# One block of modulation sums moved to VectorE, and attention scores as three reduced-precision products

## The chip, the cores and the metric

The kernel runs on one core of a Trainium2 chip. The metric is the device time of one execution in microseconds. Three executions of the kernel before took 1014.57, 1015.67 and 1015.83 us, median 1015.67.

## The reference

Two transformer blocks over one sequence of 256 rows of 1024 values, in fp32. What matters here lies at the head of the first block:

```
mod_x = silu(c) @ w_mod + b_mod            # 1024 -> 6 * 1024, one row of condition c
mod_c = silu(c_ctx) @ w_mod + b_mod        # the same for the context's condition
sh_m, sc_m, gt_m, sh_f, sc_f, gt_f = split(mod_x, 6)
hx, hc = modulate(rms_norm(x), sh_m, sc_m), modulate(rms_norm(ctx), csh_m, csc_m)
qa, ka, va, qr, kr, vr, gr = split(h @ w_in)          # for hx and for hc
att = softmax(q k^T * 64**-0.5) v                     # 8 heads of 64, 2 key heads, 256 + 256 keys
ret = bidir_retention(qr, kr, vr, decays, states of the context)
x1 = x + gt_m * rms_norm(concat(att, norm(ret) * silu(gr)) @ w_out)
x2 = x1 + gt_f * rms_norm(swiglu(modulate(rms_norm(x1), sh_f, sc_f)))
```

The first two parts of the modulation (sh_m, sc_m) are needed for both conditions before anything can be projected. The last two (sh_f, gt_f, the third group below) are needed only for `c`, and only after attention.

## The kernel before

All large products are made of a high and a low part of fp32: `w = w_hi + w_lo`, `x = x_hi + x_lo`, each part of type fp32r, and `x w` is the sum of hi·hi, hi·lo and lo·hi (function `three`, L1818 to L1820), 128x128 by 512 columns each. The weights come as 148 units of 1 MB (128 x 2048). For a unit v: SyncE loads it into one of three `raw` slots, ScalarE writes `w_hi` (L641), VectorE writes `w_lo = raw - w_hi` (L1156, called by `low_to`), TensorE uses both. A unit of `raw` is loaded again when its `w_lo` is there, and `w_hi` is written again when TensorE has used the unit.

Each engine runs a list written out by hand, and waits on semaphores; the order of the lists is the order of the work. TensorE's list after the first units is: unit W_IN+2 and +3 (values of retention, `vr`, four row tiles), +4 (`kava`: keys and values of attention), +5 and +6 (`qa`), +7 and +8 (`qr`), +9 and +10 (`gr`). Between them stand the visits of the modulation: 24 units of 1 MB of `w_mod`, in three groups of eight. `mod_unit` (L1924) multiplies one by `silu_c` (128 x 32) in plain fp32, in four strips of 512 columns that go to four column strips of the array and to 32 rows each of one PSUM bank; the trace shows each fp32 matmul as two records. Group 0 is done early, groups 1 and 2 in the visits: two units before W_IN+2's context half, then three after each of the next units, at last two; the third group is visited after the units W_IN+3 (three), W_IN+4 (three) and W_IN+5 (two). `mod_row_out` copies a group's bank, `mod_T` (L1933) transposes it, `mod_columns` (L1278) adds the bias. Twelve of these units are loaded into two places of their own (`memV`, `qrn_qan`), four through the `raw` ring.

After unit W_IN+5 TensorE makes the context's states (`states`, L2058 and L2066), which wait for `kr_done` and for four tiles of centred values (`centre_values`, L1336 to L1338, VectorE). At unit W_IN+9 it transposes the attention queries (`queries_T`, L1903), which need VectorE's two ropes over them (six ropes done in all), makes the first tile of the unit, and then the scores of the first two of eight pairs (`scores`, L2093): for each pair two fp32 matmuls, 64 rows by 128, 512 columns, key head 0 in partitions 0 to 63 and key head 1 in 64 to 127, each to its own bank. VectorE takes the maxima (L1420), ScalarE the exponentials (L834), VectorE normalises (L1432), TensorE transposes (L2217) and weights (L2168).

VectorE's list in this stretch: `w_lo` of W_IN+4; `w_lo` of W_IN+5 and W_IN+6; the block keys (L1349) and sixteen steps of decay arguments (L1354, L1358); the four centrings, with `mod_columns(1)` between; squares and norms of `ka`, `w_lo` of W_IN+7, two ropes; the states' copy (L1387); `w_lo` of W_IN+8; sums over `qa` (L1396); `w_lo` of W_IN+9; `mod_columns(2)`; norms and ropes of `qa`; `w_lo` of W_IN+10; ropes of `qr`; the first maxima. `chain` makes an instruction end before the next begins.

Of the kernel before, what the change touches and what calls it, by code (L numbers as in the profile page):

```python
# [37 lines left out]
P = 128  # L38
T = 256
# [42 lines left out]
VISITS = {W_IN + 2: 2, W_IN + 3: 3, W_IN + 4: 3, W_IN + 5: 3, W_IN + 6: 3, W_IN + 7: 2}  # L82
# [12 lines left out]
assert _m == N_MOD  # L95
STREAM += [("w", v) for v in range(W_REG, N_W)]
HEAD_UNITS = W_REG + N_MOD - MOD_K - len(OWN_MODS)
# [98 lines left out]
def plan_banks():  # L196
# [40 lines left out]
    plan.signalled(("modT", 1), 5)  # L237
    plan.streamed(("mod_row", 2), 7)
# [92 lines left out]
def two_blocks_kernel(nc, io):  # L331
# [5 lines left out]
    def sem(name):  # L337
        if name not in named:
            named[name] = sems.enter_context(nc.semaphore(name))
        return named[name]  # L340

    with sems, stack:
# [45 lines left out]
        ARENA = 18440  # L388
        spot = ExitStack()
# [8 lines left out]
        sums_r = spot.enter_context(nc.sbuf_tensor("sums_r", [P, LEVELS + 2, P], F32R))  # L398
        spot.close()
# [14 lines left out]
        qaT, kaT = carve(0, PAIRS, T), carve(1024, 4 * P)  # L414
# [24 lines left out]
        silu_gr = carve(at, TB, 512); tables = carve(at, 4, TB * HD); at += 1024  # L439
        ka_all = carve(at, 4, P); at += 512  # L440
# [57 lines left out]
        own_mods = [memV[:].rearrange("p b d -> p (b d)"), qrn_qan]  # L498
        hi_ready = sem("hi_ready")
# [70 lines left out]
        def _(sp):  # L570
# [9 lines left out]

            sp.dma_start(cols[:], io["cols"]).then_inc(sem("cols_loaded"), 16)
# [20 lines left out]
            for u in range(W_IN + 2, HEAD_UNITS):  # L602
                unit_in(u)
                kind, v = STREAM[u]
                if kind == "w" and v in VISITS:
                    for n, (m, (at, slot)) in enumerate(OWN_MODS.items()):
                        if at == v:
                            sp.wait_ge(mod_used, mods_behind(v)[0])
                            sp.dma_start(own_mods[slot], io["own_mods"][n]).then_inc(sem(f"own_mod_loaded{slot}"), 16)
                if u == RAW_AT[("w", W_IN + 2)]:  # L610
                    sp.dma_start(const1, io["const1"]).then_inc(sem("const1_loaded"), 16)
# [24 lines left out]
        def _(act):  # L636
# [85 lines left out]
            def mod_row_out(g):  # L722

                act.wait_ge(mod_used, MOD_K * (g + 1))
# [94 lines left out]
            act.activation(kaT[:, :], b[:, :], ACT.Copy).then_inc(read_sem(("kaT", 0)), 1)  # L819
# [3 lines left out]
            queries_out("qaT", qaT)  # L823
# [316 lines left out]
        def _(dve):  # L1140
# [204 lines left out]
            ins.then_inc(sem("kr_done"), 1)  # L1345
            low_to(W_IN + 5)
            low_to(W_IN + 7)
# [63 lines left out]
            dve.wait_ge(mod_used, N_MOD)  # L1411
# [3 lines left out]
            low_to(W_IN + 11)  # L1415

# [398 lines left out]
        def _(pe):  # L1815
# [111 lines left out]

            def mod_T(g):
# [159 lines left out]
            def scores(p):  # L2088
                j, tb = p // 2, p % 2
                for kv in range(KV_HEADS):  # L2090
                    half = slice(64 * kv, 64 * kv + 64)
                    b = free(pe, ("scores", p, kv))
                    pe.matmul(b[:, :], qaT[half, j, tb * P:(tb + 1) * P], kaT[half, :],  # L2093
                              start=True, stop=True).then_inc(full_sem(("scores", p, kv)), 1)
# [15 lines left out]
            for part, units, tiles in [("vr", 2, both), ("kava", 1, both), ("qa", 2, both[:2]), ("qr", 2, both[:2]),  # L2110
                                       ("gr", 2, both[:2])]:
                for e in range(units):
# [5 lines left out]
                    if j == 4:  # L2118
                        mod_T(1)
# [430 lines left out]
def lay_out(a):  # L2550
# [30 lines left out]
    for at in (512, 0, 1024, 2560, 3072, 2048, 1536):  # L2581
# [25 lines left out]
        "first_mods": np.stack(mods[:MOD_K]), "own_mods": np.stack([mods[m] for m in OWN_MODS]),  # L2607
        "cols": np.concatenate([small[name] for name in COLS], axis=1),
# [21 lines left out]
```

## Time and profile before

| what | us |
|---|---|
| median of three executions | 1015.67 |
| the profiled execution, its own time | 1015.45 |
| its span, first to last instruction | 1013.7 |
| TensorE busy (5164 matmuls) | 995.3 (98%) |
| VectorE busy (660) | 584.6 (58%) |
| ScalarE busy (603) | 495.8 (49%) |
| the chain that ended last, TensorE's share | 93% |

Busy time of TensorE is modelled: a 512-column fp32r matmul is shown as some 0.39 us long but the next one starts 0.23 us after it. The distance of starts is what a matmul costs in a dense row. The granted clock of TensorE was 0.998 of its full speed over the span.

### The profile page before, as it was taken

How to read it: one execution, taken by the hardware profiler on the slowest of the kernel's cores; microseconds unless marked ns; L12 is line 12 of the kernel's file. 1: busy time of each engine (PE TensorE's matmuls, PEld its weight loads, DVE VectorE, ACT ScalarE, POOL GpSimd, SP SyncE). 2: the span in 40 equal slices, each digit the busy share in tenths (PEclk: the TensorE clock that was granted, in tenths of full speed). 3: DMA queues.
4: the chain of work that ended last, by engine and by line, in shares of the span. 5: the costliest groups of instructions: out<-in, count | busy, mean ns of one | idle time of the engine just before them, and what ended most of it. 6: DMA issues, size and time to landing. Idle time of an engine off the chain costs nothing.

```text
span 1013.7 us, 13246 instructions
## 1 busy us (share of the span) xinstructions
PE 995.3 (98%) x5164; PEld 810.6 (80%) x5164; DVE 584.6 (58%) x660; ACT 495.8 (49%) x603; POOL 0.2 (0%) x4
## 2 busy tenths in 40 slices
PE   7999999999999999999999999999999999999997
PEld 5777776778888888888888887888888878888885
DVE  5374768667555554565555665567774465555543
ACT  6473347656544443554444534663545554444432
POOL 0000000000000000000000000000000000000000
PEclk9999999999999999999999999999999999999999
DMA  9967653133655545475545465534244245555441
GB/s 373 419 272 297 274 218 126 43 121 128 213 203 173 199 169 205 166 259 174 199 166 193 166 222 182 195 125 147 102 166 166 81 147 192 198 177 202 166 166 42
DMA packets 26686, 188.32 MB, mean 186 GB/s; under 512 B 2960, under 2 KB 3216, under 8 KB 4112
## 3 DMA queue, kind: packets, MB, share of 16 engines
q1 hardware_dynamic: 26064, 185.24, 50.2%
q10 hardware_dynamic: 576, 2.43, 0.6%
q8 instruction: 34, 0.56, 0.2%
q14 instruction: 12, 0.10, 0.0%
HBM read 186.61 MB, written 1.05 MB: 185 GB/s over the span
## 4 chain that ended last, share of the span: by engine, by line
PE 93%; DMA 2%; DVE 2%; ACT 1%; issue 1%; SPq 1%; ACTq 0%; DVEq 0%
PE bank L1818 24%; PE bank L1820 24%; PE bank L1819 24%; DMA raw<-in_weights 2%; PE bank L2026 2%; PE bank L1862 2%; PE bank L1846 2%; PE bank L1924 2%; PE bank L1854 2%; PE bank L2292 1%; PE bank L1903 1%; PE bank L2390 1%; PE bank L2217 1%; PE bank L2168 1%; PE bank L2093 1%
## 5 line engine op out<-in xcount | busy, mean ns | idle before, releaser
L1156 DVE TENSOR_TENSOR w_lo<-raw,w_hi 128x2048 fp32r<-128x2048 f32 x148 | 338.6, 2291 | 267.6 <-ACT w_hi L641 267.4
L641 ACT ACTIVATE w_hi<-raw 128x2048 fp32r<-128x2048 f32 x148 | 283.7, 1918 | 268.1 <-PE bank L1820 217.4
L1818 PE MATMUL bank<-w_hi,hT_hi 128*128 128x512 f32 (+1 forms) x760 | 299.8, 394 | 0.0
L1820 PE MATMUL bank<-w_hi,hT_lo 128*128 128x512 f32 (+1 forms) x760 | 294.9, 388 | 0.0
L1819 PE MATMUL bank<-w_lo,hT_hi 128*128 128x512 f32 (+1 forms) x760 | 294.3, 387 | 0.0
L1818 PEld LDWEIGHTS bank<-w_hi,hT_hi 128*128 128x128 f32 x760 | 142.8, 188 | 33.0 <-issue 5.7
L1820 PEld LDWEIGHTS bank<-w_hi,hT_lo 128*128 128x128 f32 x760 | 142.7, 188 | 29.8
L1819 PEld LDWEIGHTS bank<-w_lo,hT_hi 128*128 128x128 f32 x760 | 143.0, 188 | 27.8 <-issue 0.2
L1818 PE MATMUL bank<-w_hi,gT_hi 128*128 128x512 f32 x264 | 103.4, 392 | 0.0
L1820 PE MATMUL bank<-w_hi,gT_lo 128*128 128x512 f32 x264 | 102.8, 389 | 0.0
L1819 PE MATMUL bank<-w_lo,gT_hi 128*128 128x512 f32 x264 | 102.7, 389 | 0.0
L1820 PEld LDWEIGHTS bank<-w_hi,gT_lo 128*128 128x128 f32 x264 | 49.6, 188 | 10.4
L1819 PEld LDWEIGHTS bank<-w_lo,gT_hi 128*128 128x128 f32 x264 | 49.6, 188 | 10.2
L1818 PEld LDWEIGHTS bank<-w_hi,gT_hi 128*128 128x128 f32 x264 | 49.6, 188 | 10.0
L918 ACT ACTIVATE arena<-bank,rstd 128x256 f32<-128x256 f32 x44 | 18.4, 470 | 63.5 <-PE bank L1820 63.5
L1570 DVE SCALAR_TENSOR_TENSOR arena<-bank,rstd,arena 128x256 f32<-128x256 f32 x44 | 19.3, 479 | 30.8 <-ACT arena L918 30.8
L1576 DVE TENSOR_TENSOR gT_lo<-bank,gT_hi 128x512 f32 (+1 forms) x33 | 22.8, 690 | 3.2
L1846 PE MATMUL bank<-w_hi,hT_hi 128*128 128x512 f32 x88 | 22.3, 395 | 2.2 <-issue 0.8
L918 ACT ACTIVATE arena<-bank 128x256 f32<-128x256 f32 x22 | 7.2, 381 | 31.7 <-PE bank L1820 31.7
L1862 PE MATMUL bank<-w_lo,hT_hi 128*128 128x512 f32 x88 | 22.0, 392 | 0.2 <-DVE w_lo L1156 0.2
L1854 PE MATMUL bank<-w_hi,hT_lo 128*128 128x512 f32 x88 | 22.1, 393 | 0.0
L719 ACT ACTIVATE arena<-bank 128x512 f32<-128x512 f32 (+1 forms) x18 | 8.7, 553 | 27.2 <-PE bank L1820 23.8
(310 smaller groups left out, 1008.1 us busy)
## 6 DMA issues: line engine op xcount, KB each, us to landing
raw<-in_weights SPq DMA_DIRECT2D x152, 1024.0 KB, 4.8
arena<-in_first_mods SPq DMA_DIRECT2D x8, 1024.0 KB, 14.9
memV<-in_own_mods SPq DMA_DIRECT2D x6, 1024.0 KB, 4.8
arena<-in_own_mods SPq DMA_DIRECT2D x6, 1024.0 KB, 6.9
arena<-in_const ACTq DMA_DIRECT2D x1, 1088.0 KB, 5.1
memV<-in_mem SPq DMA_DIRECT2D x1, 1024.0 KB, 6.4
x_res<-in_x SPq DMA_DIRECT2D x1, 1024.0 KB, 17.5
arena<-in_ctx SPq DMA_DIRECT2D x1, 1024.0 KB, 15.2
```

Source lines behind the costliest of these rows:

```text
L641: act.activation(w_hi[:, v_slot, :], raw[:, u_slot, :], ACT.Copy).then_inc(hi_ready, 1)
L918: act.activation(gate[:, c % 3, tb, :], bank[(c % 3) * 2 + tb][:, 0:256], ACT.Silu, scale=rstd[:, tb:tb + 1] if f else 1.0)\
L1156: ins = dve.tensor_tensor(w_lo[:, v_slot, n], raw[:, u_slot, n], w_hi[:, v_slot, n].bitcast(F32), ALU.subtract)
L1576: dve.tensor_tensor(gT_lo[:, s, :], bank[6][:, :].rearrange("p (a t) -> p a t", t=T), gT_hi[:, s, :].bitcast(F32), ALU.subtract).then_inc( ...
L1818: pe.matmul(out, hi, rhi, start=start, stop=False)
L1819: pe.matmul(out, hi, rlo, start=False, stop=False)
L1820: return pe.matmul(out, lo, rhi, start=False, stop=stop)
L1846: pe.matmul(out[:, :], hT_hi[:, 2 * q + e, tb * P:(tb + 1) * P], weights(w_hi, q, e), start=(first and q == quarters[0] and e == 0), stop= ...
L1854: pe.matmul(out[:, :], hT_lo[:, 2 * q + e, tb * P:(tb + 1) * P], weights(w_hi, q, e), start=False, stop=False)
L1862: ins = pe.matmul(out[:, :], hT_hi[:, 2 * q + e, tb * P:(tb + 1) * P], weights(w_lo, q, e), start=False, stop=(last and q == quarters[1] a ...
L1924: ins = pe.matmul(b[32 * j:32 * j + 32, :], silu_c[:, k, :], w[:, 512 * j:512 * j + 512], start=(k == 0), stop=(k == MOD_K - 1))
L2026: ins = pe.matmul(out[:, :], (lo if x_low else hi)[:, 4 * half + e, tb * P:(tb + 1) * P], w[:, v % RING, e * 512:(e + 1) * 512], start=(st ...
```

## The change

The third group is no longer multiplied by TensorE unit by unit. Its 8 MB are cut into sixteen pieces of 128 x 1024 (`row_mods`: eight for the first 1024 columns, eight for the second), and VectorE multiplies each by the column `silu_c[:, k, 0:1]` and adds it to a running total (`mod_rows`); only the condition `c` is kept. Then four fp32 matmuls with a stationary of ones sum the totals over the partitions (`mod_sums`). The pieces go to four places of 512 KB (the two halves of `memV` and of `qrn_qan`), of which two hold the totals as well. The visits after W_IN+3, +4 and +5 are gone, `mod_T(1)` stands after W_IN+3 instead of W_IN+4 and has another bank.

The scores are three fp32r products of high and low parts. ScalarE writes the high parts in the copies that it made before, VectorE adds three subtractions for the low parts.

```diff
+ROW_SLOTS = [0, 1, 2, 3, 1, 2, 3, 1, 2, 3, 1, 3, 1, 3, 1, 3]
+ROW_LOADS = {W_IN + 6: 12, W_IN + 7: 4}
-    plan.signalled(("modT", 1), 5)
-    plan.streamed(("mod_row", 2), 7)
+    plan.signalled(("modT", 1), 7)
+    plan.signalled(("mod_row", 2), 7)
...
+        row_mod = [mod_sum[:, e * 1024:(e + 1) * 1024] for mod_sum in own_mods for e in range(2)]
... SyncE, behind the load of unit v
+                if kind == "w" and v in ROW_LOADS:
+                    for _ in range(ROW_LOADS[v]):
+                        step = rows_in[0]
+                        rows_in[0] += 1
+                        if row_before(step) < 0:
+                            sp.wait_ge(mod_used, 2 * MOD_K)
+                        else:
+                            sp.wait_ge(sem("mod_step"), row_before(step) + 1)
+                        sp.dma_start(row_mod[ROW_SLOTS[step]], io["row_mods"][step]).then_inc(...)
... ScalarE
-            act.activation(kaT[:, :], b[:, :], ACT.Copy).then_inc(read_sem(("kaT", 0)), 1)
+            act.activation(kaT_hi[:, :], b[:, :], ACT.Copy).then_inc(sem("kaT_hi"), 1)
-            queries_out("qaT", qaT)
+            for q in range(2):
+                b = filled(act, ("qaT", q))
+                act.activation(qaT_hi[...], b[:, :], ACT.Copy).then_inc(sem("qaT_hi"), 1)
... VectorE
+            def mod_rows(a, b):
+                for step in range(a, b):
+                    slot, part, k = ROW_SLOTS[step], step // MOD_K, step % MOD_K
+                    total = row_mod[2 * part]
+                    dve.wait_ge(sem(f"row_loaded{slot}"), 16 * row_loads(step))
+                    if k == 0:
+                        dve.tensor_scalar(total, row_mod[slot], silu_c[:, k, 0:1], None, ALU.mult).then_inc(sem("mod_step"), 1)
+                    else:
+                        dve.wait_ge(sem("mod_step"), step)
+                        dve.scalar_tensor_tensor(out=total, in0=row_mod[slot], scalar=silu_c[:, k, 0:1], in1=total,
+                                                 op0=ALU.mult, op1=ALU.add).then_inc(sem("mod_step"), 1)
             low_to(W_IN + 5)
-            low_to(W_IN + 7)
... block keys and decay arguments
+            low_to(W_IN + 6)
+            mod_rows(0, 12)
+            low_to(W_IN + 7)
             read_out(dve, ("vr", 3))
             for tile in (2, 3):
                 centre_values(tile)
-            mod_columns(1)
             for tile in (0, 1):
                 centre_values(tile)
+            mod_rows(12, ROW_STEPS)
+            mod_columns(1)
... after the queries' ropes
             low_to(W_IN + 11)
+            dve.tensor_tensor(kaT_lo[:, :], bank_of(("kaT", 0))[:, :], kaT_hi[...], ALU.subtract)...
+            for q in range(2):
+                dve.tensor_tensor(half(qaT_lo), bank_of(("qaT", q))[:, :], half(qaT_hi)..., ALU.subtract)...
... TensorE
+            def mod_sums():
+                pe.wait_ge(sem("mod_step"), ROW_STEPS)
+                b = free(pe, ("mod_row", 2))
+                for j in range(4):
+                    ins = pe.matmul(b[32 * j:32 * j + 32, :], ones[:, 0:32], row_mod[2 * (j // 2)][...512 columns...],
+                                    start=True, stop=True)
+                ins.then_inc(full_sem(("mod_row", 2)), 1)
             def scores(p):
                 j, tb = p // 2, p % 2
-                for kv in range(KV_HEADS):
-                    b = free(pe, ("scores", p, kv))
-                    pe.matmul(b[:, :], qaT[half, j, tb * P:(tb + 1) * P], kaT[half, :], start=True, stop=True)...
+                banks = [free(pe, ("scores", p, kv)) for kv in range(KV_HEADS)]
+                for n, (q_part, k_part) in enumerate([(qaT_hi, kaT_hi), (qaT_hi, kaT_lo), (qaT_lo, kaT_hi)]):
+                    for kv in range(KV_HEADS):
+                        half = slice(64 * kv, 64 * kv + 64)
+                        ins = pe.matmul(banks[kv][:, :], q_part[half, j, tb * P:(tb + 1) * P], k_part[half, :],
+                                        start=(n == 0), stop=(n == 2))
-                    if j == 4:
+                    if j == 3:
                         mod_T(1)
-                    if j < 6:
+                    if j == 2:
                         for m in mods_behind(W_IN + j + 2):
                             mod_unit(m)
+                    if j == 5:
+                        mod_sums()
```

## Rows read from the trace of the kernel before

**Rows 1.** The chain that ended last, in order of time: start us, us, what

```profile
103.06 2.71 PE bank L1924 x24
117.92 2.71 PE bank L1924 x24
126.30 2.06 PE bank L2058 x64
130.32 1.85 PE bank L1924 x16
149.72 1.09 ACT arena L719 x2
150.91 1.06 PE bank L1903 x8
154.72 1.92 PE bank L2093 x8
168.33 1.06 PE bank L2093 x4
186.99 0.65 PE bank L2227 x8
```

**Rows 2.** Timeline of VectorE: start, us, engine, line, operation, tiles [idle before <-releaser]

```profile
83.21 2.28 DVE L1156 TENSOR_TENSOR w_lo<-raw,w_hi 128x2048 fp32r<-128x2048 f32 x1
92.34 2.29 DVE L1156 TENSOR_TENSOR w_lo<-raw,w_hi 128x2048 fp32r<-128x2048 f32 x1 [6.85 <-ACT w_hi L641]
107.00 2.29 DVE L1156 TENSOR_TENSOR w_lo<-raw,w_hi 128x2048 fp32r<-128x2048 f32 x1 [12.36 <-ACT w_hi L641]
115.00 0.68 DVE L1336 TENSOR_REDUCE value_mean<-arena 128x8 f32<-128x512 f32 x1
115.71 0.17 DVE L1337 TENSOR_SCALAR value_mean<-value_mean 128x8 f32<-128x8 f32 x1
121.34 0.69 DVE L1370 TENSOR_TENSOR arena<-arena 128x512 f32<-128x512 f32 x1
149.86 0.69 DVE L1260 TENSOR_TENSOR arena<-arena 128x512 f32<-128x512 f32 x1
152.80 0.68 DVE L1253 TENSOR_TENSOR arena<-arena 128x512 f32<-128x512 f32 x1
167.03 1.29 DVE L1420 TENSOR_REDUCE row_max<-bank 128x1 f32<-128x512 f32 x2 [0.50 <-PE bank L2093]
```

**Rows 3.** Timeline of TensorE: two fp32r matmuls in a dense row

```profile
198.67 0.39 PE L1819 MATMUL bank<-w_lo,hT_hi 128*128 128x512 f32 x1
198.90 0.40 PE L1820 MATMUL bank<-w_hi,hT_lo 128*128 128x512 f32 x1
```

**Rows 4.** Timeline of SyncE's queue: when a load is issued

```profile
92.00 0.33 SPq L609 DMA_DIRECT2D memV<-in_own_mods  x1
```

**Rows 5.** DMA issues from 134 to 150: KB each, us from issue to landing

```profile
raw<-in_weights SPq DMA_DIRECT2D x2, 1024.0 KB, 4.7
```

**Rows 6.** DMA issues of the whole span, as rows 5

```profile
out<-xn SPq DMA_DIRECT2D x1, 512.0 KB, 2.7
fixed<-in_fixed SPq DMA_DIRECT2D x1, 128.0 KB, 2.2
```

**Rows 7.** VectorE's groups by form: xcount | busy us, mean ns | idle before

```profile
L1539 DVE SCALAR_TENSOR_TENSOR x_res<-arena,rstd,x_res 128x512 f32<-128x512 f32 x8 | 5.5, 748 | 0.1
L1186 DVE TENSOR_SCALAR xn<-x_res,rstd 128x1024 f32<-128x1024 f32 x2 | 1.5, 754 | 0.1
```

**Rows 8.** One stretch: its length, then busy us of PE, PEld, DVE, ACT, POOL; clock, DMA

```profile
121.34:150.59 29.25, 28.34 (x222) 22.18 (x220) 20.89 (x43) 12.42 (x17) 0.00 (x0) 1.00 0.65 252
```

**Rows 9.** Timeline of ScalarE, as rows 2

```profile
103.10 2.06 ACT L719 ACTIVATE arena<-bank 128x512 f32<-128x512 f32 x4 [7.87 <-PE bank L1820]
169.57 0.70 ACT L834 ACTIVATE arena<-bank,row_max 128x512 f32<-128x512 f32 x1
```

**Rows 10.** The warm-up's matmuls: ns min/median/max, first and last start

```profile
L1989 PE MATMUL bank<-mod_row x8: 592/1061/1222, 4.7 to 10.4; 128*128 128x512 f32 x8
```

More of the change, by code:

```diff
@@ L81 @@
 OWN_MODS = {}
-VISITS = {W_IN + 2: 2, W_IN + 3: 3, W_IN + 4: 3, W_IN + 5: 3, W_IN + 6: 3, W_IN + 7: 2}
+VISITS = {W_IN + 2: 2, W_IN + 3: 3, W_IN + 4: 3}
+ROW_STEPS = 2 * MOD_K
+ROW_SLOTS = [0, 1, 2, 3, 1, 2, 3, 1, 2, 3, 1, 3, 1, 3, 1, 3]
+ROW_LOADS = {W_IN + 6: 12, W_IN + 7: 4}
 W_REG = W_OUT + 2
@@ L398, in two_blocks_kernel @@
         sums_r = spot.enter_context(nc.sbuf_tensor("sums_r", [P, LEVELS + 2, P], F32R))
+        spot.close()
+        qaT_hi = spot.enter_context(nc.sbuf_tensor("qaT_hi", [P, PAIRS, T], F32R))
+        kaT_hi = spot.enter_context(nc.sbuf_tensor("kaT_hi", [P, 4 * P], F32R))
+        kaT_lo = spot.enter_context(nc.sbuf_tensor("kaT_lo", [P, 4 * P], F32R))
+        spot.enter_context(nc.sbuf_tensor("below_qaT_lo", [P, KA_ALL - 2048], F32))
+        qaT_lo = spot.enter_context(nc.sbuf_tensor("qaT_lo", [P, PAIRS, T], F32R))
         spot.close()
@@ L498, in two_blocks_kernel @@
         own_mods = [memV[:].rearrange("p b d -> p (b d)"), qrn_qan]
+        row_mod = [mod_sum[:, e * 1024:(e + 1) * 1024] for mod_sum in own_mods for e in range(2)]
+        row_before = lambda step: max([n for n in range(step) if ROW_SLOTS[n] == ROW_SLOTS[step]], default=-1)
+        row_loads = lambda step: sum(ROW_SLOTS[n] == ROW_SLOTS[step] for n in range(step + 1))
         hi_ready = sem("hi_ready")
@@ L609, in _ @@
                             sp.dma_start(own_mods[slot], io["own_mods"][n]).then_inc(sem(f"own_mod_loaded{slot}"), 16)
+                if kind == "w" and v in ROW_LOADS:
[6 more added lines that the diff above has]
+                            sp.wait_ge(sem("mod_step"), row_before(step) + 1)
+                        sp.dma_start(row_mod[ROW_SLOTS[step]], io["row_mods"][step]).then_inc(sem(f"row_loaded{ROW_SLOTS[step]}"), 16)
                 if u == RAW_AT[("w", W_IN + 2)]:
@@ L722, in mod_row_out @@
             def mod_row_out(g):
[L724 removed]
+                if g == 2:
+                    filled(act, ("mod_row", 2))
+                else:
+                    act.wait_ge(mod_used, MOD_K * (g + 1))
                 if g:
@@ L1415, in _ @@
             low_to(W_IN + 11)
+            dve.wait_ge(sem("kaT_hi"), 1)
+            dve.tensor_tensor(kaT_lo[:, :], bank_of(("kaT", 0))[:, :], kaT_hi[:, :].bitcast(F32), ALU.subtract).then_inc(read_sem(("kaT", 0)), 1)
+            for q in range(2):
+                dve.wait_ge(sem("qaT_hi"), q + 1)
+                half = lambda v: v[:, 2 * q:2 * q + 2, :].rearrange("p a t -> p (a t)")
+                dve.tensor_tensor(half(qaT_lo), bank_of(("qaT", q))[:, :], half(qaT_hi).bitcast(F32), ALU.subtract)\
+                    .then_inc(read_sem(("qaT", q)), 1)
             def negative_max(p):
@@ L1926, in mod_unit @@
                 ins.then_inc(mod_used, 1)
+            def mod_sums():
+                pe.wait_ge(sem("mod_step"), ROW_STEPS)
+                b = free(pe, ("mod_row", 2))
+                for j in range(4):
+                    ins = pe.matmul(b[32 * j:32 * j + 32, :], ones[:, 0:32], row_mod[2 * (j // 2)][:, j % 2 * 512:j % 2 * 512 + 512],
+                                    start=True, stop=True)
+                ins.then_inc(full_sem(("mod_row", 2)), 1)
             def mod_T(g):
@@ L2089, in scores @@
                 j, tb = p // 2, p % 2
-                for kv in range(KV_HEADS):
-                    half = slice(64 * kv, 64 * kv + 64)
-                    b = free(pe, ("scores", p, kv))
-                    pe.matmul(b[:, :], qaT[half, j, tb * P:(tb + 1) * P], kaT[half, :],
-                              start=True, stop=True).then_inc(full_sem(("scores", p, kv)), 1)
+                banks = [free(pe, ("scores", p, kv)) for kv in range(KV_HEADS)]
[4 more added lines that the diff above has]
+                                        start=(n == 0), stop=(n == 2))
+                        if n == 2:
+                            ins.then_inc(full_sem(("scores", p, kv)), 1)
             def first_scores():
@@ L2607, in lay_out @@
         "first_mods": np.stack(mods[:MOD_K]), "own_mods": np.stack([mods[m] for m in OWN_MODS]),
+        "row_mods": np.stack([f("w_mod")[0][k * P:(k + 1) * P, 2 * UNIT + c:2 * UNIT + c + 1024] for c in (0, 1024) for k in range(MOD_K)]),
         "cols": np.concatenate([small[name] for name in COLS], axis=1),
```

13 lines of the change are left out of this document (9 added, 4 removed).

## The prediction

> **What bounds the kernel now.** I read the page's busy shares first: TensorE 98% of the span, VectorE 58%. The chain of waits agrees; in order of time it is one piece of TensorE work after another around the change [rows 1], with one pause: at 149.72 TensorE waits 1.2 us for ScalarE's copies before it transposes the queries at 150.91. So TensorE's work counts one for one as long as nothing else becomes late. VectorE's timeline [rows 2] is the second view: it waits 6.85 us before 92.34 and 12.36 us before 107.00, both times for `w_hi`, but from 107 to 121.34 it has no gap. The DMA view and SyncE's timeline [rows 4 to 6] come third, since the change puts sixteen loads in line behind VectorE's own steps. So the question is whether 19 us of VectorE's idle time hold the new work before its list comes up behind TensorE's.
>
> **TensorE's work.** The visits removed are 2.71, 2.71 and 1.85 us on the chain [rows 1]: 7.27. `mod_sums` has the form of one unit (four fp32 matmuls in four column strips, eight records); three units take 2.71, so one is 0.90. Saved: 6.37.
>
> Scores: a pair in fp32 takes 1.06 on the chain (x4 in rows 1), eight pairs. New are six fp32r matmuls of 512 columns on half the rows each. In a dense row one starts 0.23 after the other (198.67, 198.90 [rows 3]). No row shows fp32r on half the rows, so both bounds: if the two halves run side by side, three by 0.23 and the 0.2 by which a pair is longer than its streaming now (two records of 2 x 0.215 each take 0.86 of the 1.06), 0.89; if they don't, six by 0.215 and 0.2, 1.49. The nearest rows are fp32 on half rows: eight records with 128 columns take 0.65 in L2227, against 1.06 for the eight full-array ones of L1903 [rows 1], so halves do overlap there. I take 0.89: 8 x 0.17 = 1.4 saved (other bound: 3.4 lost).
>
> The Trainium skill, "TensorE: Matmul & The Clock Gate", part 3 on packing small matmuls, says that matmuls in different row groups run at the same time but for a few ns; it gives no fp32r case. By it a pair is 0.89, without it 1.49, and the rows above, in fp32, are on its side.
>
> Together 7.8 us less work: 1007.7, if nothing waited.
>
> **VectorE's new steps.** Fourteen multiply-adds over 128x1024 with a pointer scalar. The same form at 512 is 0.748 [rows 7]; 512 elements more cost 512/1536 of the difference between 2048 and 512 elements (2.29 and 0.69 [rows 2]), 0.53: 1.28. Each waits for the one before; a chained pair has 0.03 between end and start (115.00, 115.71 [rows 2]): 1.31. Two first steps of a half are scalar multiplies of 128x1024, 0.754 [rows 7], 0.78 with the gap. Sum 14 x 1.31 + 2 x 0.78 = 19.9.
>
> **The loads.** A lone load of 1 MB lands 4.7 after its issue [rows 5]. 128 KB take 2.2 [rows 6]; the line between them gives 3.3 for 512 KB, and 4.7 less half of the streaming (1 MB at some 420 GB/s is 2.5) gives 3.45. I take 3.45. Bounds: 2.7, the 512 KB store [rows 6], and 4.7, if half the size saved nothing. The first four may go when group 1 is used up, where the own loads went before, 92.00 [rows 4]; they land at 95.45, 96.7, 97.95, 99.2. Every later load waits until its place's last step is done, so a place comes round in 1.31 + 3.45 + 0.1 for the hand-overs = 4.9, while three steps are 3.9 long and two are 2.6. For steps 4 to 8 three places turn, at the end two.
>
> **VectorE's new timeline.** `w_lo` of W_IN+4 as before, 83.21. Block keys and decay arguments (115.00 - 107.00 - 2.2 = 5.8 [rows 2]) now stand ahead of the next wait, in idle time: free. `w_lo` of W_IN+5 at 92.34, to 94.6. Twelve steps: 10 x 1.31 + 2 x 0.78 = 14.7, and waits for landings of 0.8 and 0.5 at the start, then 1.0, 1.0, 0.5, 1.0 and 1.3 before steps 4, 7, 9, 10 and 11: 6.1. End 115.4. `w_lo` of W_IN+6 to 117.7 (its `w_hi` is there since 107). Centring 6.1 (115.00 to 121.34 less 0.2 for the columns [rows 2]): 123.8. Four steps 5.2; the load of step 14 is issued after step 12, so 2.3 of wait: 131.3, columns 131.5. Before, this point was 121.34. From there to the ropes' end (149.86 + 0.69, before `w_lo` at 150.59) VectorE is busy 20.9 of 29.25 [rows 8], and some 0.5 are gaps between chained steps. Now all it needs is there when it comes (W_IN+7 and +8 too, although SyncE issues their loads behind the pieces: +7 at 111, +8 at 127, landed by 132.5, `w_lo` wanted at 140.6). So 131.5 + 21.4 = 152.9.
>
> **TensorE's new timeline.** W_IN+3 ends at 103.0 as before; `mod_T(1)` 0.44; then W_IN+4 waits for bank 4, whose copy starts at 103.10 [rows 9] and was covered by the visit: 0.4 lost. W_IN+4 and +5 end at 121.2. The states (126.30 before [rows 1]) want the centred values: 123.8, 2.6 lost. States and transposes 4.0: 127.8. `mod_sums` wants step 16 and the bank that `mod_columns(1)` frees: 131.6, 3.7 lost. By then 6.7 of the 7.3 are gone, and the 0.9 are to be paid: TensorE begins W_IN+6 at 132.5, before 132.17. It reaches the queries' transposes at 150.2 plus ScalarE's 1.2, but the ropes end at 152.9: 153.0 against 150.91, +2.1.
>
> **After that.** `w_lo` of W_IN+10 (2.2) and three new subtractions over 512 (2.1) end at 157.2; TensorE wants them for the scores at 156.9: 154.72 becomes 157.2, +2.5, and two shorter pairs make it +2.1. VectorE's list however is 4.4 late now (152.80 becomes 157.2). The maxima of pair 2 (167.03 [rows 2]) come at 171.0, its exponentials end at 173.9 instead of 170.27 [rows 9], and the scores of pair 4 need those banks: +3.5. The four pairs left give 0.7 back, the rest is TensorE's as before. With some 0.3 of slack that the later steps still have, I take +2.5 at the end. Nothing behind 190 absorbs it, TensorE's chain is dense there.
>
> Sum on the profiled execution: 1015.45 - 7.8 + 10.3 of new waits (0.4, 2.6, 3.7, 1.6 more at the ropes, 0.4, and 1.6 in attention) = 1017.95. That execution lies 0.2 under the median of 1015.67; I forecast 1018.0. A tenth of a us in the landing is worth 0.5 us: five round trips stand in VectorE's path.
>
> **Rivals.** *The loads keep up (faster).* If a piece lands in 2.7 us, as the 512 KB store does, the waits in VectorE's path shrink by 3.8 and the end is at 1014.2; at 2.0 us at 1011, and with no waits at all (7.1 less) VectorE reaches the ropes' end at 145.8, TensorE is the bound at 145, and the end is near 1009.7. It decides below about 2.9 us. For it: VectorE's 19 us of idle time. Against it: the line through rows 5 and 6. I give 1012.5 as its time.
>
> *The halves don't run side by side in fp32r.* A pair is 1.49: 0.6 x 8 = 4.8 more work, of which some is hidden where VectorE is late anyway (first two pairs, and part of the third): +3.0, 1021.0. Against it: L2227 in fp32.
>
> *The clock falls.* Nowhere after 12 us does TensorE wait longer than the 1.2 us at 149.72. Now it waits 3.7 at a stretch before `mod_sums`, and 2.6 just before. In the warm-up the same matmul takes 1061 to 1222 ns at the low level (1.2 GHz), and 592 at the high one (2.4 GHz), for some 4.6 us, after an idle 4.7 us [rows 10]. 4.6 us at half speed lose 2.3: 1020.3. Against it: the waits are short, with dense work between. The Trainium skill, "TensorE: Matmul & The Clock Gate", section on why this matters, warns of idle gaps between bursts that put the array back to half rate; by it this case is likelier than the rows alone make it, and no run here has tried.
>
> **How the numbers follow.** Forecast 0.54, loads keep up 0.19, halves serial 0.15, clock 0.12. The forecast's own range, landing 3.1 to 4.0, is 1016.0 to 1020.8. The range for all: down into the first rival, 1011.5, up past the second, 1022.0; beyond it are landings over 4.2 or two mishaps, and below it a landing under 2. A difference under 0.2% (2.0 us) can't be told from none. Faster: the first rival but for its upper end, 0.18. Within: that end, and 0.25 of the forecast's lower half, 0.29 with 0.01 elsewhere: 0.30. Slower: 0.52.
>
> **What would show it.** Right: in the timeline of VectorE steps of about 1.28 with gaps before every third one, the last at 130 to 132; TensorE idle before L2058 and before the four matmuls of `mod_sums`, released by VectorE; the queries' transposes at 153, released by a rope. L2093's pairs 0.9 apart from their neighbours. Wrong: steps without gaps, or landings of the 512 KB pieces under 2.9; a granted clock under 1.00 after 127; pairs of 1.5.

## The result, and the profile after

The changed kernel takes 1021.61 us (median of 4 runs, 1021.2 to 1022.0); the kernel before, with a fourth execution beside the three, 1015.25 (1014.57 to 1015.83). The ratio is 1.0064, its 95% interval 1.0051 to 1.0077: slower, at the upper end of the forecast's range, 3.6 us above its 1018.0. The profiled execution has a span of 1020.0 against 1013.7: 6.3 more. Of all executions below one, of e9_half_columns_first, was disturbed (1432.63 us at a granted clock of 0.655), and its comparison leaves it out.

The page's busy shares come first again. VectorE has 20 us more work, as worked out (584.6 before), and TensorE 5.4 less (995.3 before):

```profile
PE 989.9 (97%) x5124; PEld 812.2 (80%) x5124; DVE 605.0 (59%) x679; ACT 496.0 (49%) x603; POOL 0.2 (0%) x4
PE 85%; DVE 7%; DMA 4%; ACT 2%; issue 1%; SPq 1%; DVEq 0%; ACTq 0%
```

The second line is the share of each engine in the chain of waits. TensorE had 93% of it; now VectorE and the DMAs stand in it with 11% (4% before). In order of time, the chain leaves TensorE at 92 us and comes back to it only at 177.27 [rows 1]. These are its DMAs and the point where it comes back:

```profile
93.10 6.05 DMA arena<-in_row_mods
101.87 5.09 DMA arena<-in_row_mods
108.30 4.21 DMA arena<-in_row_mods
113.85 3.33 DMA arena<-in_row_mods
129.41 4.57 DMA arena<-in_row_mods
177.27 0.96 PE bank L2155 x6
```

Each of these transfers is one 512 KB piece from its issue to the sum that wants it. Between them and behind them the chain is VectorE's list, and from 165 us on the maxima and ScalarE's exponentials with it. VectorE's timeline shows the sums (L1382 the first step of a half, L1385 the others) with the waits that end on them. For [rows 2] it has, over the same stretch:

```profile
96.14 0.75 DVE L1382 TENSOR_SCALAR memV<-memV,silu_c 128x1024 f32<-128x1024 f32 x1 [1.19 <-DMA memV<-in_row_mods]
104.11 1.28 DVE L1385 SCALAR_TENSOR_TENSOR memV<-arena,silu_c,memV 128x1024 f32<-128x1024 f32 x1 [0.87 <-DMA arena<-in_row_mods]
106.99 1.28 DVE L1385 SCALAR_TENSOR_TENSOR memV<-arena,silu_c,memV 128x1024 f32<-128x1024 f32 x1 [1.60 <-DMA arena<-in_row_mods]
...
117.20 1.28 DVE L1385 SCALAR_TENSOR_TENSOR arena<-arena,silu_c 128x1024 f32<-128x1024 f32 x1 [1.99 <-DMA arena<-in_row_mods]
...
132.20 1.28 DVE L1385 SCALAR_TENSOR_TENSOR arena<-memV,silu_c,arena 128x1024 f32<-128x1024 f32 x1 [2.82 <-DMA memV<-in_row_mods]
134.00 1.28 DVE L1385 SCALAR_TENSOR_TENSOR arena<-arena,silu_c 128x1024 f32<-128x1024 f32 x1 [0.51 <-DMA arena<-in_row_mods]
135.20 0.18 DVE L1308 TENSOR_TENSOR mod<-bank,cols 128x32 f32<-128x32 f32 x1
```

Behind the first sum VectorE waits 10.9 us for pieces in all. Behind the last sum come the columns at 135.20, and 0.2 later the step L1415, which stood at 121.34 (L1370 [rows 2]): 14.1 us later. The page's DMA issues say how long a piece takes, as medians:

```profile
arena<-in_row_mods SPq DMA_DIRECT2D x9, 512.0 KB, 4.6
memV<-in_row_mods SPq DMA_DIRECT2D x7, 512.0 KB, 4.2
```

Single ones take 3.2 to 6.8 us, and what sets them apart is what else is on its way. SyncE's timeline has the issues:

```profile
100.48 1.72 SPq L633 DMA_DIRECT2D arena<-in_row_mods  x2
103.26 0.33 SPq L633 DMA_DIRECT2D memV<-in_row_mods  x1
113.85 0.33 SPq L633 DMA_DIRECT2D arena<-in_row_mods  x1
```

The piece of 113.85 is issued with nothing else under way and lands in 3.3 (the chain above has it). The second of 100.48 goes at 101.87, 1.39 behind one piece and 1.39 ahead of the next, and takes 5.1; the next, at 103.26 with both still on their way, takes 4.9. The one of 128.02 again has nothing ahead of it, but another piece and 2 MB of weights close behind, and takes 4.2. As long as VectorE does not wait it frees a place every 1.39 us, so two or three reloads are mostly on their way at once.

TensorE's timeline shows what that costs there, in brackets the idle time ahead:

```profile
104.20 0.35 PE L1870 MATMUL bank<-w_hi,hT_hi 128*128 128x256 f32 x1 [0.45 <-ACT arena L743]
126.90 3.63 PE L2119 MATMUL bank<-arena 128*64 128x64 f32 x64 [5.48 <-issue]
131.40 1.09 PE L1955 MATMUL bank<-fixed,arena 128*128 128x128 f32 x8
135.53 0.62 PE L1985 MATMUL bank<-memV,fixed 128*32 128x512 f32 x2 [3.04 <-DVE mod L1308]
144.59 0.47 PE L1870 MATMUL bank<-w_hi,hT_hi 128*128 128x512 f32 x1 [1.88 <-issue]
157.43 1.06 PE L1955 MATMUL bank<-fixed,arena 128*128 128x128 f32 x8 [1.22 <-ACT arena L743]
173.45 1.06 PE L2283 MATMUL bank<-fixed,arena 128*128 128x128 f32 x8 [0.45 <-ACT arena L743]
177.27 0.50 PE L2155 MATMUL bank<-kaT_hi,qaT_hi 64*128 64x512 f32 x2 [0.83 <-ACT arena L864]
```

Without the 1.22, which was there before, these are 12.1 us of new waits. 5.5 of them are for the centred values (the view says "issue"; the centring ends at 126.8). The states' matmuls then take 3.63 instead of 2.06 [rows 1], and from there to the transposes at 131.40 are 4.50 us where it was 2.99 (126.23 to 129.22 in the timeline of before): 1.5 lost at the low clock. 12.1 + 1.5 - 7.8 of work saved (as forecast) is 5.8 of the 6.3; the other 0.5 has no place here. TensorE's clock and its 1.88 stand in this sum, but e4_filled_waits and e3_four_loads show below that they do not set the time.

### The profile page after: what moved, and what is told of

It reads as the page before. It is cut to its first block, busy times and chain, and to the rows that moved or that the text cites. A ratio compares the mean times of both kernels' runs of the same rounds, so it can differ in the third digit from the quotient of the medians.

```text
span 1020.0 us, 13216 instructions
## 1 busy us (share of the span) xinstructions
PE 989.9 (97%) x5124; PEld 812.2 (80%) x5124; DVE 605.0 (59%) x679; ACT 496.0 (49%) x603; POOL 0.2 (0%) x4
## 4 chain that ended last, share of the span: by engine, by line
PE 85%; DVE 7%; DMA 4%; ACT 2%; issue 1%; SPq 1%; DVEq 0%; ACTq 0%
PE bank L1870 22%; PE bank L1872 22%; PE bank L1871 22%; DMA arena<-in_row_mods 2%; DMA raw<-in_weights 2%; PE bank L2087 2%; PE bank L1914 2%; PE bank L1898 2%; PE bank L1906 2%; DVE w_lo L1186 2%; PE bank L2358 1%; PE bank L2456 1%; PE bank L1976 1%; PE bank L1955 1%; PE bank L2234 1%
## 5 line engine op out<-in xcount | busy, mean ns | idle before, releaser
L1870 PEld LDWEIGHTS bank<-w_hi,hT_hi 128*128 128x128 f32 x760 | 142.8, 188 | 33.6 <-issue 6.4
L1898 PEld LDWEIGHTS bank<-w_hi,hT_hi 128*128 128x128 f32 x88 | 16.3, 188 | 6.5 <-issue 2.5
```

Source lines behind the costliest of these rows:

```text
L1870: pe.matmul(out, hi, rhi, start=start, stop=False)
L1898: pe.matmul(out[:, :], hT_hi[:, 2 * q + e, tb * P:(tb + 1) * P], weights(w_hi, q, e), start=(first and q == quarters[0] and e == 0), stop= ...
```

## The experiments

**e1_rows_only**: the changed kernel with fp32 scores as before, so only the row sums are new.

```diff
-                banks = [free(pe, ("scores", p, kv)) for kv in range(KV_HEADS)]
-                for n, (q_part, k_part) in enumerate([(qaT_hi, kaT_hi), (qaT_hi, kaT_lo), (qaT_lo, kaT_hi)]):
...
+                    pe.matmul(b[:, :], qaT[half, j, tb * P:(tb + 1) * P], kaT[half, :], start=True, stop=True)...
```

> The changed kernel with the scores of before (two fp32 matmuls a pair, no subtractions for low parts); the row sums stay. Theory V: VectorE's list sets the time from the sixteen sums on, so its three subtractions (2.1 us) cost more than the shorter pairs give back: scores of pair 4 start about 2 us earlier than in the changed kernel (177.3), the later pairs are 0.17 longer each: 1020.3, 1 to 1.5 us under the changed kernel (1021.6). Rival T: TensorE's work counts, eight pairs longer by 0.17: 1023.0.

Measured: 1021.15 us, ratio to before 1.0057 (1.0044 to 1.0071), between the two theories and within the noise of the changed kernel. The loss is the row sums'.

**e2_scores_only**: the kernel before with the three-product scores alone (the same lines the other way round).

> The kernel before with only the scores changed to three fp32r products. Theory V: VectorE has little slack at that place even before; the ropes of qr start 2 us later, the maxima of pair 2 1.4 later, the scores of pair 4 1.0 later, and the pairs after it give 0.7 back: 1015.5, no measurable difference to 1015.25. Rival T: 8 x 0.17 saved, 1013.9.

Measured: 1015.14 us, ratio 1.0003 (0.9994 to 1.0012): no difference. TensorE's timeline shows the halves side by side (x2 in a row: the two halves of one product), and a pair's start 0.76 behind the last one's:

```profile
154.69 0.50 PE L2111 MATMUL bank<-kaT_hi,qaT_hi 64*128 64x512 f32 x2 [0.33 <-DVE qaT_lo L1431]
155.00 0.42 PE L2111 MATMUL bank<-kaT_lo,qaT_hi 64*128 64x512 f32 x2
...
155.45 0.43 PE L2111 MATMUL bank<-kaT_hi,qaT_hi 64*128 64x512 f32 x2
```

What the pairs save is gone again on VectorE: its three subtractions stand ahead of the maxima, the first of which comes at 158.45 instead of 157.04.

**e3_four_loads**: the changed kernel without 12 of the 16 piece loads (that part of the computation is left out): the first load of each place stays, and the sums run over what lies there.

```diff
+                        if row_before(step) >= 0:
+                            continue
...
-                    dve.wait_ge(sem(f"row_loaded{slot}"), 16 * row_loads(step))
+                    dve.wait_ge(sem(f"row_loaded{slot}"), 16)
```

> The changed kernel with only the first four of the sixteen pieces loaded; the other twelve sums take what lies in their place, so the third group of the modulation is computed from wrong pieces (that part of the computation is left out). All VectorE, TensorE and ScalarE instructions stay. Theory V: the waits for landings in the sums (10.9 us in the changed kernel's VectorE timeline behind the first sum) are what makes it slower: the sixteenth sum ends at 124 instead of 135, the queries' transposes come at about 147 instead of 157.4, the time is 1011 to 1012. Rival W: VectorE's 20 us of sums themselves are too much: then the transposes stay above 151 and the time above 1016.

Measured: 1012.3 us, ratio 0.9970 (0.9958 to 0.9982). With no landing to wait for behind the first four, the last sum ends at 125.4 instead of 135.3, and in the profiled execution the granted clock stays at 1.00 from 90 to 160 us. VectorE's arithmetic itself is affordable; its waits are not. But 1012.3 is not 1009.7, the price that the prediction gave to "no waits at all". TensorE's timeline has a wait that looks like the reason:

```profile
103.82 0.35 PE L1872 MATMUL bank<-w_hi,hT_hi 128*128 128x256 f32 x1 [0.45 <-ACT arena L745]
125.59 0.62 PE L1987 MATMUL bank<-memV,fixed 128*32 128x512 f32 x2 [0.53 <-DVE mod L1310]
134.65 0.47 PE L1872 MATMUL bank<-w_hi,hT_hi 128*128 128x512 f32 x1 [1.90 <-issue]
```

The 1.9 are the same as in the changed kernel, and the prediction does not have them: W_IN+8 wants two banks that ScalarE copies out, and ScalarE's copies wait for the keys' ropes, which now come right behind the last sum on VectorE. ScalarE's timeline (of e3_four_loads) has the wait and its releaser:

```profile
132.50 0.60 ACT L840 ACTIVATE arena<-bank 128x512 f32<-128x512 f32 x1 [2.01 <-DVE arena L1292]
```

So between `mod_sums` and the fourth rope VectorE is the longer of the two engines even if the sums come early. And it stays so: after the 0.52 us ahead of its second sum at 97.22, VectorE's timeline has no idle time until

```profile
167.29 0.17 DVE L1483 RECIPROCAL row_inv<-row_sum 128x2 f32<-128x2 f32 x1 [0.19 <-ACT arena L866]
```

The chain of e3_four_loads too is VectorE's and ScalarE's up to 167.33, where the scores of pair 4 begin. TensorE's 1.9 lies beside that path, and 1012.3 is what VectorE's own list costs, with its three new subtractions. In the profiled executions the time from `mod_columns(1)` to the end is the same in the changed kernel (columns at 135.20), here (125.26), in e4_filled_waits (134.83), e5_half_pieces (128.06) and e12_two_row_halves (143.45), 886.5 to 886.7 us, and 887.3 to 887.4 in e6_centre_first and e10_two_halves. So the time of each is set by when VectorE gets there.

**e4_filled_waits**: the changed kernel with nine idle-filling matmuls, five ahead of the states and four ahead of `mod_sums`, into a bank that is free there. Nothing is left out.

```diff
+            def keep_busy(n):
+                b = free(pe, ("qr", 0))
+                for _ in range(n):
+                    pe.matmul(b[:, :], mod_row[:, 0:P], mod_row[:, :], start=True, stop=True)
```

> The changed kernel with nine more fp32 matmuls of 512 columns into an unused bank, five ahead of TensorE's wait for the centred values and four ahead of its wait for the sums, so that it is busy where it stood idle and its granted clock should stay at the high level (1.00 from 122 to 131 instead of 0.5 to 0.7). Theory V: the low clock cost nothing, since what TensorE lost there (1.6 us in the states) it would have waited for the sums: 1021.6, within 0.7. Rival C: the low clock is part of the loss: 2 us faster, 1019.6.

Measured: 1021.41 us, ratio 1.0061 (1.0048 to 1.0075): nothing gained. The busy times by stretch of the changed kernel show the low clock, those of this one show none up to 136 (columns: length, busy us of PE, PEld, DVE, ACT, POOL; clock, DMA share, GB/s). First the changed kernel:

```profile
122.00:126.00 4.00, 0.00 (x0) 0.00 (x0) 3.83 (x9) 1.79 (x2) 0.00 (x0) 0.69 0.00 1
126.00:128.00 2.00, 1.10 (x21) 1.13 (x23) 1.96 (x3) 0.00 (x0) 0.00 (x0) 0.50 0.04 8
128.00:130.00 2.00, 2.00 (x43) 2.00 (x42) 1.28 (x1) 0.00 (x0) 0.00 (x0) 0.50 0.41 125
130.00:132.00 2.00, 2.00 (x50) 1.93 (x46) 0.00 (x0) 0.00 (x0) 0.00 (x0) 0.92 0.75 236
```

Then e4_filled_waits:

```profile
122.00:126.00 4.00, 4.00 (x22) 1.77 (x22) 3.86 (x8) 0.64 (x1) 0.00 (x0) 1.00 0.00 0
126.00:130.00 4.00, 4.00 (x100) 3.69 (x96) 1.94 (x2) 0.00 (x0) 0.00 (x0) 1.00 0.50 146
136.00:140.00 4.00, 4.00 (x14) 3.05 (x11) 3.93 (x9) 3.50 (x5) 0.00 (x0) 0.57 0.39 90
```

The states run at full speed, and `mod_sums` waits for VectorE all the same. The clock then falls behind the second wait (2.1 us), and VectorE's ropes end at 156.2, where they ended at 156.5. What TensorE does at half speed ahead of a point that VectorE sets costs nothing. A wait alone does not say whether the clock will fall: in the changed kernel it stays at 1.00 after the 3.04 us ahead of `mod_sums`.

**e5_half_pieces**: each load brings 128x512 instead of 128x1024; the sums keep their width (so half of each is left out of the computation).

```diff
-                        sp.dma_start(row_mod[ROW_SLOTS[step]], io["row_mods"][step])...
+                        sp.dma_start(row_mod[ROW_SLOTS[step]][:, 0:512], io["row_mods"][step])...
```

> The changed kernel with each of the sixteen piece loads cut from 128 x 1024 to 128 x 512 elements (256 KB instead of 512 KB); VectorE's sums still run over 1024 columns, so half of each sum is over what already lies in the place (that part of the computation is left out). Theory F (a piece's landing is mostly a slow start that every load pays, 4.2 to 4.6 us for 512 KB beside 4.7 for 1 MB): landings fall by less than 0.5 us each, and with five round trips on VectorE's list the time falls by 1 to 2 us, to about 1020. Theory S (landing follows the size, as in the prediction's estimate from 2.2 us for 128 KB, 2.7 for a 512 KB store and 4.7 for 1 MB, 2.5 us for each MB between the ends): landings fall by 0.6 us or more and the time by 3 us, to about 1018.5. If landings reach 2.9 us or less, the sums are no longer waiting and the time is near that with four loads, 1012.3.

Measured: 1014.74 us, ratio 0.9998 (0.9990 to 1.0007), 6.9 below the changed kernel: neither theory, and more than both. The landings say why:

```profile
arena<-in_row_mods SPq DMA_DIRECT2D x9, 256.0 KB, 3.1
memV<-in_row_mods SPq DMA_DIRECT2D x7, 256.0 KB, 3.0
```

They fell by 1.2 to 1.5 us, not by 0.5 or 0.6, and the columns behind the last sum come at 128.06 instead of 135.20, 7.1 earlier: the first sum starts 1.1 earlier, and the waits behind it are 4.5 instead of 10.9. That is 0.5 for each tenth of a us in the landing, as the prediction has it. Size alone does not give the 1.4: pieces issued with nothing else under way, or with others about to land, take 3.2 to 3.3 us for 512 KB (98.73 and 113.85 in the changed kernel, 101.19 in e7_half_group) and 2.7 for 256 KB (97.17 here), 0.5 to 0.6 apart, near the 0.7 of the line through [rows 5, 6]. The rest goes with the crowd: with one or two others on their way the halved pieces still land in 2.7 to 3.1 (97.17 to 104.20), the whole ones mostly in 3.6 to 5.1. This is read from rows; no run spaces whole pieces out.

**e6_centre_first**: VectorE's list reordered, six sums, then the centring, then the other ten.

```diff
-            mod_rows(0, 12)
-            low_to(W_IN + 7)
+            mod_rows(0, 6)
             read_out(dve, ("vr", 3))
...
-            mod_rows(12, ROW_STEPS)
+            low_to(W_IN + 7)
+            mod_rows(6, ROW_STEPS)
```

> The changed kernel with VectorE's list in another order: the first six of the sums, then the centring of the values, then the low half of the weight after next, then the other ten sums. Nothing is left out. Theory V (VectorE's list with the landings it waits for sets the time): the landings that fall into the centring (6 us of it) are hidden, some 3 us of waits go, and the time falls to about 1018.5; TensorE's wait of 5.5 us ahead of the states and its low clock go as well, but that by itself gives nothing. Theory T (TensorE's own waits and the low clock are the loss): the 5.5 us and 2 to 3 us of low clock come back in full, 1014 to 1016.

Measured: 1024.14 us, ratio 1.0081 (1.0068 to 1.0094). Both theories failed: it is 2.5 above the changed kernel, though the two intervals overlap. The states' wait is gone, but the views of TensorE's waits and of VectorE's timeline show a larger one in its place:

```profile
PE bank L1985 <- DVE mod L1308: 13.0, 1, 13.0
```

```profile
128.62 1.28 DVE L1385 SCALAR_TENSOR_TENSOR arena<-memV,silu_c,arena 128x1024 f32<-128x1024 f32 x1 [4.02 <-DMA memV<-in_row_mods]
133.30 1.28 DVE L1385 SCALAR_TENSOR_TENSOR arena<-memV,silu_c,arena 128x1024 f32<-128x1024 f32 x1 [2.01 <-DMA memV<-in_row_mods]
```

The centring can hide only as many landings as there are places, which it did before too; and all the sums with two places turning now stand behind it in one row, with W_IN+7's load of 1 MB, issued at 120.32, in the same DMA queue as they are: the piece issued at 122.23 behind it takes 6.4. The waits behind the first sum come to 14.6 us instead of 10.9.

**e7_half_group**: from the kernel before. VectorE sums k = 0 to 3 (eight pieces), TensorE goes on visiting k = 4 to 7 from the weights' ring and adds the four matmuls of `mod_sums` to the same bank.

```diff
+VISITS = {W_IN + 2: 2, W_IN + 3: 3, W_IN + 4: 3}
+LATE_MODS = [W_IN + 5, W_IN + 6, W_IN + 7, W_IN + 8]
+ROW_K = 4
+ROW_SLOTS = [0, 2, 1, 3, 1, 3, 1, 3]
... VectorE
+            mod_rows(0, 6)
+            low_to(W_IN + 7)
             read_out(dve, ("vr", 3))
...
-            mod_columns(1)
             for tile in (0, 1):
                 centre_values(tile)
+            mod_rows(6, ROW_STEPS)
+            mod_columns(1)
```

> The kernel before with only half of the third group moved: VectorE sums the rows k = 0 to 3 (8 pieces, 8 sums), TensorE goes on visiting k = 4 to 7 and adds the one matmul pair over VectorE's sums; the scores stay in fp32. Nothing is left out. Theory V (what the full change costs is VectorE's time and waits beyond its idle time, what it brings is TensorE's visits): TensorE is relieved of 4 visits of 0.9 us and does 0.9 more, 2.7 us, and VectorE's 10 us with its landings fit into what it has idle before the ropes: 1012.3, 1011.5 to 1013.5. Theory R (any row sum on VectorE delays the centring or the ropes by as much as it saves): 1015 or more.

Measured: 1018.15 us (1016.5 to 1020.5), ratio 1.0037 (1.0024 to 1.0050). The expected gain is not there. The profiled execution is the fastest of the five (1016.50, against 1015.45 before), so most of the loss is in no trace. TensorE's waits in this stretch:

```profile
PE bank L1854 <- DVE mod L1299: 2.4, 1, 2.4
PE bank L1939 <- ACT arena L740: 1.2, 1, 1.2
PE bank L1978 <- ACT mod_row L740: 0.8, 1, 0.8
```

The 1.2 was there before; the 0.8, ahead of `mod_T(2)`, is new. L1299 is `mod_columns(1)`, which also frees a bank. It comes at 118.77, where VectorE's timeline of before has it at 118.06, and TensorE, with fewer visits, wants that bank sooner.

**e8_half_group_scores**: the same with the three-product scores.

> The kernel e7_half_group with the change's scores as three products of high and low parts. Nothing is left out. Theory V: as on the kernel before, where this part alone gave 1.0003, VectorE's extra halves take back what the shorter pairs give: within 1 us of e7_half_group, about 1012.3. Rival G (the pairs' 8 times 0.17 us come through once VectorE is not late): 1.4 us below e7_half_group, about 1011.

Measured: 1019.52 us, ratio 1.0041 (1.0027 to 1.0055). The intervals of the two overlap: again nothing from the scores. Its profiled execution (1019.39) has 4.1 for the wait at that bank, and a granted clock of 0.79 from 118 to 126 us.

**e9_half_columns_first**: e7_half_group with `mod_columns(1)` ahead of the last two sums.

```diff
-            mod_rows(6, ROW_STEPS)
             mod_columns(1)
+            mod_rows(6, ROW_STEPS)
```

> e7_half_group with mod_columns(1) ahead of VectorE's last two sums instead of behind them. Nothing is left out. Theory B (e7_half_group lost its gain because the columns' bank, which TensorE wants behind W_IN+5, came free only behind both sums, a wait of 2.4 us at L1854): that wait goes, and the time falls by 2.4 us, to about 1015.7, or to the median of before at 1015.2. Rival R (what holds it up are the pieces' landings, whose place does not matter to TensorE at that point): within 0.7 us of e7_half_group, 1018.

Measured: 1015.39 us (median of eleven runs), ratio 1.0004 (0.9995 to 1.0013), 2.8 below e7_half_group where theory B has 2.4. The size fits better than the trace: in the profiled executions the bank wait goes from 2.4 only to 1.1, and they are 0.3 apart (1016.50 and 1016.16). It is level with the kernel before, not faster. Its pieces land in 7.0 us (6.9 in the other row), since the weights' loads stand ahead of them in the queue.

**e10_two_halves** and **e12_two_row_halves**: the changed kernel with two loads for each piece, by columns (128x512) and by rows (64x1024). **e11_half_two_halves**: e9_half_columns_first with the halves by columns.

```diff
-                        sp.dma_start(row_mod[ROW_SLOTS[step]], io["row_mods"][step])...
+                        for h in range(2):
+                            cut = slice(512 * h, 512 * h + 512)
+                            sp.dma_start(row_mod[ROW_SLOTS[step]][:, cut], io["row_mods"][step][:, cut])...
```

> The changed kernel with each piece loaded by two DMAs of 128 x 512 elements one behind the other on SyncE, instead of one of 128 x 1024; the sum waits for both. Nothing is left out. Theory L (a lone load moves its data slowly whatever its size, and two at once overlap): a pair lands 0.4 us behind one of 256 KB (3.05 in e5_half_pieces), about 3.5 instead of 4.2 to 4.6; with five round trips the time falls by 4 to 5 us, to about 1017. Theory E (the engines' rate for these packets sets it): the pair lands in 4.4 us or later, 1021.6 or more.

> The changed kernel with each piece loaded by two DMAs of 64 rows x 1024 elements, so the packets keep their length. Nothing is left out. Theory L: as e10_two_halves, about 1017. Theory E, or 64 rows spread over fewer of the engines: no gain, 1021.6 or more. The difference from e10_two_halves tells what the length of the packets is worth.

> e9_half_columns_first with each piece loaded by two DMAs of 128 x 512 elements. Nothing is left out. Theory L: landings that VectorE waits for are shorter by up to 1 us, but only two round trips stand in its path there: 0 to 1.5 us below e9_half_columns_first. Theory E: as e9_half_columns_first or up to 1 us above it, for the longer time of issue on SyncE.

Measured: 1023.66 us, ratio 1.0084 (1.0069 to 1.0099), for the halves by columns; 1030.19, ratio 1.0151 (1.0137 to 1.0164), for the halves by rows; 1017.03, ratio 1.0020 (1.0011 to 1.0029), for e11. Theory L fell: none of the three gained. By columns the time is 2.0 us above the changed kernel, with intervals that overlap; by rows it is 8.6 above, clear of noise; e11 is 1.6 above e9_half_columns_first, and the intervals just overlap. The landings in the first two, columns first, then rows:

```profile
arena<-in_row_mods SPq DMA_DIRECT2D x18, 256.0 KB, 4.1
memV<-in_row_mods SPq DMA_DIRECT2D x14, 256.0 KB, 3.6
```

```profile
arena<-in_row_mods SPq DMA_DIRECT2D x18, 256.0 KB, 4.9
memV<-in_row_mods SPq DMA_DIRECT2D x14, 256.0 KB, 4.7
```

By columns a half lands 0.6 to 1.0 later than the single halves of e5_half_pieces (3.0 to 3.1), and the second is issued 0.4 later. The pair of 127.47, with nothing ahead of it, shows it plainly: the first half lands in 3.0, the second in 5.0, so the two overlap, but the piece is complete after 5.4 where the whole one of 128.02 took 4.2. By rows the same bytes hold the DMA engines fully and move more slowly still, from 94 to 100 us (last columns: clock, DMA share, GB/s; the changed kernel moves 325 at a share of 0.90 there):

```profile
94.00:100.00 6.00, 6.00 (x28) 4.97 (x27) 2.27 (x3) 1.25 (x5) 0.00 (x0) 1.00 1.04 244
```

## Why the prediction came out as it did

*TensorE's work.* Right. The visits and `mod_sums` are as worked out; the two halves of a product run side by side in fp32r: the second pair starts 0.76 behind the first, and the chain of the changed kernel has 0.89 for a pair with its hand-over, as forecast, where it had 1.06 [rows 1] and halves in a row would be 1.49:

```profile
180.28 0.89 PE bank L2155 x6
```

The rival "halves don't run side by side" is out. That the scores bring nothing, the forecast says only in part: it charged VectorE's subtractions but kept some gain; e2_scores_only measured 1.0003.

*VectorE's new steps.* 0.75 and 1.28 us, as worked out. Two in a row without a wait start 1.39 apart (106.99 and 108.38), not 1.31; five or so such pairs stand there, 0.4 us.

*The landing: the term that was mis-sized.* 3.45 was taken; the medians are 4.2 and 4.6, with single ones from 3.2 to 6.8. For a piece alone 3.45 was a good price: those with nothing else under way, or nearly so, take 3.2 to 3.3. What the sum left out is that a place comes free every 1.39 us, so that each reload travels with one or two others, and the first four, issued within 1.3 us, land in 3.9 to 6.8. The first sum starts 0.7 later than forecast, and the waits behind it are 10.9 instead of 7.6 (the forecast's 8.4 less the 0.8 ahead of the first sum): the last sum ends at 135.3, not 131.3. The step behind the columns comes at 135.42 instead of 131.5, 3.9 late, and the end is 3.8 late (1021.76 against 1017.95), so the whole miss lies ahead of that step. From it to the ropes' end are 21.0 us, where 21.4 was taken.

That the time still lies within the forecast's range is in part luck. The prediction puts landings over 4.2 beyond its upper end, and with 4.4 its own rule gives 1022.7, past 1022.0; 1021.6 was measured, since a tenth of a us was worth 0.4 here and not 0.5. The upper end had been set by the halves in a row, which did not come. e5_half_pieces bears the rule out; e3_four_loads shows where it ends.

The Trainium skill, "DMA: Bandwidth & Descriptors", section on the anatomy of one DMA, fits a transfer issued from GpSimd by 2.0 us and 436 GB/s; estimates from it are 3.2 for a piece and 2.6 for 256 KB. The traces here, with SyncE as the issuer, agree for loads that are alone or nearly so: 3.2 to 3.3 (98.73, 113.85), and 2.7 (97.17 in e5_half_pieces). Where others are on their way they have 3.6 to 5.7 for a piece, and with 2 MB close behind 4.2 for a piece (128.02) and 3.3 for 256 KB (122.15 in e5_half_pieces): there the measurement decides.

*TensorE's new waits.* The first, 0.4, is there (0.45). The states' was 5.5 and not 2.6, `mod_sums`' 3.0 and not 3.7, that in attention 1.3 and not 2.0. The 1.6 more that the prediction puts at the queries' transposes, "released by a rope", are not there: these come at 157.43, not 153, behind ScalarE's two copies and the same 1.22 as before. TensorE had waited earlier, 1.9 ahead of W_IN+8, for ScalarE's copies behind the fourth rope, which the prediction passed over; both ways it follows VectorE.

*VectorE behind the ropes.* The prediction has the maxima of pair 2 at 171.0, and they come at 174.24: VectorE's list is 7.8 late at the ropes of `qr` (160.58 against 152.80), 7.2 at the maxima, and the end is 6.3 late. That this list sets the time through attention is right. But the far end of "loads keep up", 1009.7, drops it: there the prediction makes TensorE the bound, although by its own terms VectorE, with 2.1 us of subtractions behind the ropes, would be only some 2.7 us ahead of before. e3_four_loads measured 1012.3, with VectorE's list 2.2 ahead at the ropes of `qr` (150.57).

*The clock.* The rival's mechanism came, its price did not. In the 5.5 us without work ahead of the states TensorE's granted clock falls to 0.50, the lower of its two levels (1.2 GHz), and it is back at 1.00 by 132. The Trainium skill, "TensorE: Matmul & The Clock Gate", section on why this matters, warns of idle gaps between bursts of matmuls. The trace agrees on this gap; the one of 3.0 us ahead of `mod_sums`, at which the rival had looked, leaves the clock at 1.00. And e4_filled_waits takes the low clock out of that stretch, and the time stays (1021.41).

*The rival that loads keep up.* The prediction lets it decide below about 2.9 us, where its line is level with before. Pieces of 256 KB, at 3.0 to 3.1, come out at 1014.7, level with before; the line has 1016 there. So the point lies near, 0.1 to 0.2 us above where the prediction put it.

What stays open: what in the queue or the engines makes loads that travel together slow each other down before the engines are full (from 99 to 113 us their busy share is 0.70 to 0.95), why the piece of 128.02 takes 4.2 with nothing ahead of it (2 MB of weights are issued close behind), and why halves by rows are so much slower. A run of the changed kernel with its reloads spaced out would settle the first.

## What to carry to other kernels

Work moved to an idle engine is paid in that engine's round trips, not in its arithmetic: here VectorE's 20 us of sums alone were affordable (1012.3), and the waits for reloaded places, 10.9 us in all, made 1012.3 into 1021.6. A reload's price from a row of a load that travels alone is too low where the steps free places faster than loads land: count how many will be on their way at once, and take a row with as many, or the slow end. And when an engine gets work ahead of a shared list, ask at every later point which engine's list is the longer one, also where the moved work itself has long been done, and follow every bank that a moved step frees.

## What the runs showed of the hardware

A load of 512 KB from SyncE's queue lands in 3.2 to 3.3 us if nothing else is under way (101.19 in e7_half_group, 113.85 in the changed kernel), and in 3.6 to 5.7 if others were on their way (the other pieces from 100.48 to 118.51 in the changed kernel); 1 MB takes 4.7 [rows 5]. One of 256 KB takes 2.7 to 3.1 with one or two others on their way (97.17 to 104.20 in e5_half_pieces). Two of 256 KB for one piece land later than one of 512 KB, above all if cut by rows (1030.2 against 1021.6 us for the kernel, 244 GB/s at a DMA share of 1.04). fp32r matmuls on 64 rows each run two at a time (0.89 us for a pair of scores, six matmuls). TensorE's granted clock fell to 0.50 within 5.5 us without work, stayed at 1.00 after 3.0, and in e4_filled_waits fell after a wait of 2.1.
